# Value products of the sparse heads written to alternate halves of the PSUM partitions, four key tiles per job

## The reference

```python
def dsa_block(q, k, v, q_idx, k_idx, w_idx, q_pos, slopes, topk):
    ...
    top_val, top_idx = lax.top_k(score, kk)
    ...
    v_sel = jax.vmap(lambda vb, ib: vb[ib])(v, top_idx)
    logits = jnp.einsum('bqhd,bqkd->bhqk', q, k_sel).astype(jnp.float32) * (B_DH ** -0.5)
    ...
    p = jax.nn.softmax(logits, axis=-1)
    o = jnp.einsum('bhqk,bqkd->bqhd', p.astype(v_sel.dtype), v_sel)
```

## Time and profile before

| what | value |
|---|---|
| time, median of 3 runs | 4198.86 us (4189.95 to 4199.72) |
| profiled execution: span | 4197.5 us, mean granted clock 0.924 |
| PE busy over the span | 3628.2 us (86%) |
| DVE, ACT busy | 2294.2 us (55%), 1778.7 us (42%) |
| attention stage | about 1460 to 2462 us |

### The profile page before, as it was taken

How to read it: one execution, slowest core, us unless ns; L and a number is a source line. 1 busy time by engine, 2 the same in 40 slices (tenths; PEclk the granted TensorE clock), 3 DMA queues, 4 the chain that set the end, 5 groups by cost and what they waited for, 6 DMA issues and landing times. The chain is left out here.

```text
span 4197.5 us, 46254 instructions
## 1 busy us (share of the span) xinstructions
PE 3628.2 (86%) x16604; PEld 2834.2 (68%) x16604; DVE 2294.2 (55%) x4283; ACT 1778.7 (42%) x2978; POOL 167.9 (4%) x298
## 2 busy tenths in 40 slices
PE   8598977779875389999999969779999999999998
PEld 3476755557663256666676648668888877888886
DVE  1421777777777355655555537644545455544545
ACT  0321777767776266665565543222111122112112
POOL 0000000011010010000000000000000000000000
PEclk9699888889886589999999989989999999999999
DMA  7323212222222343111101024431111133111111
GB/s 281 116 95 114 67 60 68 68 80 87 74 90 87 99 139 90 54 40 35 37 27 31 16 87 157 149 125 52 40 60 40 57 88 115 40 60 40 40 60 50
DMA packets 262990, 327.15 MB, mean 78 GB/s; under 512 B 22434, under 2 KB 196034, under 8 KB 262532
## 3 DMA queue, kind: packets, MB, share of 16 engines
q1 hardware_dynamic: 240292, 251.69, 18.9%
q0 software_dynamic: 22528, 73.30, 5.0%
HBM read 238.83 MB, written 86.07 MB: 77 GB/s over the span
## 5 line engine op out<-in xcount | busy, mean ns | idle before, releaser
L1556 PE MATMUL p<-m_h_hi,w_hi 128*128 128x512 f32 x1024 | 401.7, 392 | 47.9 <-DVE m_h_lo L1485 35.5
L721 PE MATMUL isps<-ki,iq_hi 128*128 128x512 f32 (+3 forms) x608 | 260.4, 429 | 196.3 <-ACT spare L753 165.5
L1469 DVE TENSOR_TENSOR total<-p,total 128x1024 f32<-128x1024 f32 x256 | 313.2, 1223 | 204.3 <-PE p L1571 202.5
L1571 PE MATMUL p<-w_hi,a_hi 128*128 128x512 f32 x1024 | 401.2, 392 | 17.1 <-DVE w_lo L1443 8.8
L760 ACT ACTIVATE below<-rank,tk 128x2048 int8<-128x2048 f32 (+13 forms) x294 | 383.4, 1305 | 57.3 <-DVE tk L851 46.3
L1556 PE MATMUL p<-m_h_lo,w_hi 128*128 128x512 f32 x1024 | 401.0, 392 | 0.0
L1556 PE MATMUL p<-m_h_hi,w_lo 128*128 128x512 f32 x1024 | 400.8, 391 | 0.0
L1571 PE MATMUL p<-w_lo,a_hi 128*128 128x512 f32 x1024 | 400.7, 391 | 0.0
L1571 PE MATMUL p<-w_hi,a_lo 128*128 128x512 f32 x1024 | 400.4, 391 | 0.0
L822 DVE SCALAR_TENSOR_TENSOR rank<-spare,iw,rank 128x1024 f32<-128x1024 f32 (+5 forms) x330 | 332.9, 1021 | 83.9 <-ACT spare L753 79.6
L753 ACT ACTIVATE spare<-isps 128x1024 f32<-128x1024 f32 (+5 forms) x352 | 280.9, 811 | 154.2 <-PE isps L721 77.4
(11 more groups left out here) (212 smaller groups left out, 7125.3 us busy)
## 6 DMA issues: line engine op xcount, KB each, us to landing
w_raw<-in_w_ff SPq DMA_DIRECT2D x64, 1024.0 KB, 6.2
ada_w<-in_w_ada SPq DMA_DIRECT2D x12, 2048.0 KB, 8.9
q_hi<-dram_proj_hi SPq DMA_DIRECT2D x128, 128.0 KB, 3.0
q_lo<-dram_proj_lo SPq DMA_DIRECT2D x128, 128.0 KB, 3.1
iq_hi<-dram_proj_hi SPq DMA_DIRECT2D x224, 64.0 KB, 2.4
iq_lo<-dram_proj_lo SPq DMA_DIRECT2D x224, 64.0 KB, 2.4
dram_proj_hi<-r_ev_hi POOLq DMA_DIRECT2D x52, 256.0 KB, 3.1
dram_proj_lo<-r_ev_lo POOLq DMA_DIRECT2D x52, 256.0 KB, 3.4
```

The lines of the kernel that those rows point to most:

```text
L721: mm = nc.tensor.matmul(sps[:, job.n % 2, a:b], q[:, job.unit % IQU, job.head % 2, :], ki[:, job.c * SCH + a:job.c * SCH + b], start=part ...
L1469: nc.vector.tensor_tensor(total[:, t, :], p2[:, t % 2, :], total[:, t, :], ALU.add).then_inc(s_t, 1)
L1556: mm = nc.tensor.matmul(p1[:, u, :], a[:, k, f * P:(f + 1) * P], b[:, k, g * GT:(g + 1) * GT], start=i == 0, stop=i == 3 * KT - 1)
L1571: mm = nc.tensor.matmul(p2[:, t % 2, d * GT:(d + 1) * GT], a[:, slot, f, t * P:(t + 1) * P], b[:, f, d * GT:(d + 1) * GT], start=i == 0, s ...
```

## The change

The two heads' 64 value rows fill half the PSUM partitions. Now even key tiles accumulate in partitions 0 to 63 of `ops` and odd ones in 64 to 127 (`half = kt % 2 * DH`). `out` copies all 128 partitions to `ot` (64 where a group has one tile). The two halves must be added: `back` is no longer a transpose of 64 rows but a float32 product of `ot` (stationary, 128x128 for each head) with `stack`, two 64x64 identities one over the other, which turns and adds at once. `stack` is made by two small copies on ACT at the start of the stage, and PE waits for them.

A `pv` job now holds four key tiles, sparse and dense, and waits for the copies of both pairs. There are four `pt` buffers instead of two, and a copy into one waits for the `pv` job that read it last. The planner's cost of a sparse `pv` job is 0.15 + 0.27 us per tile.

```diff
 SCH = 1024
 QU = 3
+PT = 4
...
-                pv = add("pv", Job("pv", "PE", 0.43 * tiles, where, group,
-                                   [turned] + ([groups[n - 2].out] if k == 0 and n >= 2 else []), first=k,
-                                   tiles=tiles, of=turn, last=k + 2 >= group.tiles, pv=n_pv))
+                n_slot += 1
+                if k % 4 == 0 and k + 2 < group.tiles:
+                    continue
+                first = k - k % 4
+                tiles += k - first
+                cost = 0.15 + 0.27 * tiles if group.sparse else 0.43 * tiles
+                pv = add("pv", Job("pv", "PE", cost, where, group,
+                                   [turned] + ([groups[n - 2].out] if first == 0 and n >= 2 else []), first=first,
+                                   tiles=tiles, of=turn, slot=n_slot - (2 if first < k else 1), pv=n_pv))
                 n_pv += 1
+                reader += [pv] * (n_slot - len(reader))
...
-            if job.kind == "turned" and job.pv >= 2:
-                after.append(streams["pv"][job.pv - 2])
+            if job.kind == "turned" and job.reader:
+                after.append(job.reader)
...
-        pt = sb("pt", [P, 2, GT])
-        ot = sb("ot", [DH, 2 * P])
+        pt = sb("pt", [P, PT, GT])
+        ot = sb("ot", [P, 2 * P])
+        stack = sb("stack", [P, DH])
...
             def _(pe):
+                pe.wait_ge(s_id, 2)
...
-                        slot = job.of.pv % 2
                         for kk in range(job.tiles):
                             kt = job.first + kk
+                            slot, at = (job.slot + kk // 2) % PT, kk % 2
                             if g.sparse:
-                                mm = nc.tensor.matmul(ops[0:DH, g.n % 2, 0:2 * P], vb[:, kt, :],
-                                                      pt[:, slot, kk * 2 * P:(kk + 1) * 2 * P],
-                                                      start=kt == 0, stop=kt == g.tiles - 1)
+                                half = kt % 2 * DH
+                                mm = nc.tensor.matmul(ops[half:half + DH, g.n % 2, 0:2 * P], vb[:, kt, :],
+                                                      pt[:, slot, at * 2 * P:(at + 1) * 2 * P],
+                                                      start=kt < 2, stop=kt >= g.tiles - 2)
...
+                        rows = DH if g.tiles == 1 else P
                         for hh in range(2):
-                            tr = nc.tensor.transpose(tps[:, job.turn % 2, hh * DH:(hh + 1) * DH],
-                                                     ot[:, hh * P:(hh + 1) * P], keep.ident[0:DH, 0:DH])
+                            tr = nc.tensor.matmul(tps[:, job.turn % 2, hh * DH:(hh + 1) * DH],
+                                                  ot[0:rows, hh * P:(hh + 1) * P], stack[0:rows, :],
+                                                  start=True, stop=True)
...
+                for half in range(2):
+                    rows = slice(half * DH, (half + 1) * DH)
+                    nc.scalar.activation(stack[rows, :], keep.ident[rows, rows], ACT.Copy).then_inc(s_id, 1)
...
-                            nc.scalar.activation(ot[:], ops[0:DH, g.n % 2, 0:2 * P], ACT.Copy).then_inc(s_oe, 1)
+                            rows = DH if g.tiles == 1 else P
+                            nc.scalar.activation(ot[0:rows], ops[0:rows, g.n % 2, 0:2 * P], ACT.Copy).then_inc(s_oe, 1)
```

More of the change, by code:

```diff
@@ L1601, in __init__ @@
         self.of, self.pv, self.on_act = fields.get("of"), fields.get("pv"), fields.get("on_act")
+        self.slot, self.reader = fields.get("slot"), None
 class Group:
@@ L1626, in attention_streams @@
                    bias=[])
-    hm = n_head = n_group = n_pv = 0
+    hm = n_head = n_group = n_pv = n_slot = 0
+    reader = []
     units, groups, masks, reads = 0, [], {}, {}
@@ L1691, in attention_streams @@
                 where = n + 1 + k / group.tiles
-                turn = add("turn", Job("turn", "PE", 0.22 * tiles, where, group, ready, first=k, tiles=tiles, pv=n_pv))
+                turn = add("turn", Job("turn", "PE", 0.22 * tiles, where, group, ready, first=k, tiles=tiles, slot=n_slot))
                 turned = add("turned", Job("turned", "ACT", 0.2 + 0.25 * tiles, where, group, [turn], first=k,
-                                           tiles=tiles, of=turn, pv=n_pv))
+                                           tiles=tiles, of=turn, slot=n_slot))
                 turn.of = turned
-                pv = add("pv", Job("pv", "PE", 0.43 * tiles, where, group,
-                                   [turned] + ([groups[n - 2].out] if k == 0 and n >= 2 else []), first=k,
-                                   tiles=tiles, of=turn, last=k + 2 >= group.tiles, pv=n_pv))
+                n_slot += 1
[7 more added lines that the diff above has]
+                                   tiles=tiles, of=turn, slot=n_slot - (2 if first < k else 1), pv=n_pv))
                 n_pv += 1
+                reader += [pv] * (n_slot - len(reader))
             group.turns = turn
@@ L1707, in attention_streams @@
         reads[i] = last_read
+    for job in streams["turned"]:
+        job.reader = reader[job.slot - PT] if job.slot >= PT else None
     return streams
@@ L1872, in attention @@
         s_io = sem("s_iota")
+        s_id = sem("s_stacked")
         with nc.Block() as block:
@@ L1991, in _ @@
                                     mm = nc.tensor.matmul(ops[:, g.n % 2, hh * P:(hh + 1) * P],
-                                                          pt[:, slot, (2 * kk + hh) * P:(2 * kk + hh + 1) * P],
+                                                          pt[:, slot, (2 * at + hh) * P:(2 * at + hh + 1) * P],
                                                           va[:, kt, head * P:(head + 1) * P],
@@ L2016, in _ @@
                         act.wait_ge(s_t, job.of.turn + 1)
-                        if job.pv >= 2:
-                            act.wait_ge(s_pv, job.pv - 1)
+                        if job.reader:
+                            act.wait_ge(s_pv, job.reader.pv + 1)
                         width = job.tiles * 2 * P
-                        nc.scalar.activation(pt[:, job.pv % 2, 0:width], tps[:, job.of.turn % 2, 0:width],
+                        nc.scalar.activation(pt[:, job.slot % PT, 0:width], tps[:, job.of.turn % 2, 0:width],
                                              ACT.Copy).then_inc(s_te, 1)
```

## The result

The changed kernel takes 4089.3 us (median of 4 runs, 4088.4 to 4097.3) against 4198.1 us for the kernel before: a ratio of 0.9748, 95% interval 0.9734 to 0.9762. Measured once more beside the last experiment it gave 4092.4 us (ratio 0.9761, 0.9745 to 0.9778).

What follows compares the result with a forecast made beforehand. The prediction took PE to bound the attention stage. Its terms, -84 + 15 - 8 + 8 = -69 us, against the profiled 4197.5 gave 4128.5, adjusted to 4131 us (-1.6%), with an 8-in-10 range of 4098 to 4203 us.

Steps and rivals of the forecast that it cites:

- What bounds the kernel: Attention stage: PE is the bound, busy 843.6 of 902 us from 1560 us; time taken off it should come off the stage.
- the last test of the prediction: Attention stage: the forecast is wrong if DVE's wait for PE's turns does not fall from 180 us.
- Rival E: Attention stage: halves overlap with the load bare, but ACT can't follow and PE starves; 4164 us, chance 0.08.
- The pair of tiles: Sparse value products: an even and an odd tile cost 0.53 us instead of 0.86; 256 pairs save 84 us.
- The load for B1 starts with A2: Sparse products: the odd tile's first load starts with the even tile's second pass, so its stream starts 0.05 us behind that.
- rival B: Sparse products: full overlap, a pair takes 0.43 us, saving 110 us; 4104 us (4098 to 4120), chance 0.16.
- The wait for the second copy, +15: Four-tile value jobs wait for both `pt` copies, 86 of 240 right behind their last turn: 15 us more, ends 0 and 49.
- Fewer changes of form, -8: Entering and leaving the sparse products' array form: 41 fewer runs at 0.19 us save 8 us, ends 0 and 8.
- The new back, +8: `back`, 64 times: 0.44 us instead of 0.27, 11 us, less some form changes on the way in: 8 us more.
- `out` over 128 partitions and the start: `out` copy stays at 0.375 us, and key loads hide the two start copies and PE's wait for them: zero each.
- C: Sparse products: the array takes one half at a time, a pair stays at 0.86 us; 4199 to 4214 us, chance 0.13.
- D: Sparse products: no overlap, each change of half costs 0.05 to 0.09 us; 4220 to 4250 us, chance 0.11.

Runs made afterwards that it cites:

- split_wait: The changed kernel, but a four-tile value job first waits only for its first pair's copy, and for the second's between its second and third product: 4069.8 us, ratio 0.9706.
- by_jobs: The changed kernel, but the half goes by the job (key tiles 0 to 3 lower, 4 to 7 upper, and so on): 4184.0 us, ratio 0.9978.
- old_jobs: The kernel before (its job order, two-tile jobs, two `pt` buffers) with only the halves, wide `out` and new `back` added: 4110.8 us, ratio 0.9802.
- by_pairs: The changed kernel, but two tiles in a row go to one half and the next two to the other: 4092.4 us, ratio 0.9760.

## Why the prediction was wrong

*What bounds the kernel*: right. PE's time came off the stage nearly one to one (115 - 12 of sparse products and `back`, and the stage lost 108). DVE's wait for PE's turns fell from 180 to 115, as the last test of the prediction asked. Rival E did not come: ACT waits for PE 154 us still.

*The pair of tiles*: the step that failed. "The load for B1 starts with A2" took a rule seen where all products use the same columns and carried it to a case that the rows did not show. The loads of the changed kernel, beside the products from 2230.83 us:

```profile
2230.83 0.63 PEld L2001 LDWEIGHTS ops<-pt,vb 128*64 128x64 f32 x8
```

Eight loads stand within 0.63 us, against 1.49 before. Their start times show the rule holding within each half and not across: in one half a load starts at 2231.098 behind a product at 2231.097, in the other at 2231.105 behind one at 2231.103. The load of one half doesn't wait for the other half's product. A pair costs 0.43 us, as rival B said. Term: -84 forecast, 256 x 0.43 = 110 by the rows. The upper end had been named rightly, but the value was chosen on a reading of order in a queue, and the range, which ended at 4098, had no room for the full overlap together with a second term of zero.

*The wait for the second copy, +15*: wrong too, as a difference. The wait is real (`split_wait` gained 19.5 us by lifting it), but I set the whole of it against the change and took off only a part for what the kernel before paid at the same places. The earlier trace rows showed it paid there, 0.25 us behind two turns. For one place its size was right: 0.32 us at the median sparse place of either kernel. It fell by 12 us, as the places fell from 114 to 92; and waits ahead of turns rose by about as much (in turn to turn from 12 to 21 us, in score to turn by 2 or 3). Net zero in place of +15. The waits between turns come with the new list: from turn to turn PE takes 162 us in all before, 172 in `by_jobs`, 173 in the changed kernel and 174 in `split_wait`. So they are not the waits for products in another place.

*Fewer changes of form, -8*: right as far as it can be told; 115 us of sparse products less 107 to 110 for the pairs leaves 5 to 8. The list did more than that, and the sum had no term for it. With the halves alone (`old_jobs`) the stage lost 87 us, where 110 less 14 for `back` would be 96; on top of that the list gained 21.

*The new back, +8*: it measured +12. Four records of L2019 take 0.55 us in the timeline above, 0.49 us a `back` with what stands behind it by the table (31.6/64), against 0.30 (19.3/64).

*`out` over 128 partitions and the start*: right at zero. The copy in the changed kernel:

```profile
2229.02 0.38 ACT L2048 ACTIVATE ot<-ops 128x256 f32<-128x256 f32 x1 [0.52 <-PE ops L2001]
```

takes the 0.375 us of before. The key loads' 17.7 us cover the start.

With these terms put right the sum would have been -110 + 0 - 8 + 12 = -106, 4093 us. Rival B's own price, 4104, missed by the 15 us of the second term. C and D are out: all 256 pairs overlap in the start times, C would have been some 10 us above `by_jobs`, and `by_pairs` shows that a change of half costs nothing.

## What to carry to other kernels

Where a product fills only half of the columns, send alternate products to the two halves of the PSUM partitions and add the halves in a step that runs once a group anyway; here the overlap was worth 95 us of some 4,190. Let the product that signals the end of a job be the last to start in either half; the end of this text shows why. When a change moves a wait, count the same wait in the kernel before, place by place, before charging it. When jobs are merged, let the merged job wait for its first input and take the wait for the last one in its middle: here that alone was 20 us.

## What the runs showed of the hardware

Products in different column halves ran fully side by side, at 0.215 us for two records of 256 columns, both float32, with no price for the second stream of operands nor for going from one half to the other. PE also started products of the other half ahead of the program's order. In `by_pairs` the first record of the second half started 13 ns behind the first of four in the first half, three of which had still to start. In 15 of the 16 long runs of `by_jobs`, where eight records of one half stand ahead, it started 6 or 7 ns behind the fifth, so again past three, and once behind the sixth. No run shows it passing more than three; whether that is the limit is open, since in `by_jobs` a wait of its own stands ahead of it.

By the starts of the records a semaphore's count can then come out of order too. In the run of ten records above, the record that carries the second job's increment of `s_pv` started at 1592.49 us, the last one of the first job at 1592.87. Where alternate products take alternate halves, as in the changed kernel, the last record is still the last to start, by 6 or 7 ns.
